# Two neighbouring DMA sums in GpSimd's queue change places, four times in a streaming encoder step

## The chip, the cores and the metric

One Trainium2 chip, one of its cores. The metric is the device time of one execution of the whole program in microseconds; lower is better. Before the change the median of three runs is 2460.01 us (2455.98 to 2460.65).

## The reference

One inference step of a two-layer streaming encoder over 640 tokens: 512 of a new prompt and 8 streams of 16. Layer A is half a SwiGLU step, differential attention, half a SwiGLU step; layer B the same with forgetting attention. All is float32.

```
def swiglu(x, w_gate, w_up, w_down):
    return (jax.nn.silu(x @ w_gate) * (x @ w_up)) @ w_down
...
x = x + 0.5 * swiglu(rms_norm(x, g_norm[l, 0]), w_ffn_gate[l, 0], w_ffn_up[l, 0], w_ffn_down[l, 0])
...
x = x + 0.5 * swiglu(rms_norm(x, g_norm[l, 2]), w_ffn_gate[l, 1], w_ffn_up[l, 1], w_ffn_down[l, 1])
```

D_MODEL is 1024 and D_FF 2816, so there are four such feed-forward stages, f = 0 to 3, each with three weight matrices of 11.5 MB. The change touches these stages alone.

## The kernel before

**Tiling.** The 2816 hidden columns are taken in 11 pairs of 128-column blocks, in groups of 2, 3, 3 and 3 pairs (`GROUPS`, g = 0 to 3). A group's work is a row of *sets* (g, s). Its first `width(g)` = 2 × pairs sets are gate (s even) and up (s odd) weights of one pair; then come four *down* sets (s = width(g) + 0 to 3), each for 256 of the 1024 output columns. For g = 0 the width is 4, so the down sets are (0,4) to (0,7), and (0,7) is followed by (1,0), the first gate set of the next group. `chain(f)` (L85) lists all sets in order. f = 0 starts at (0,2), and the last group of f = 3 has its down step in another form (`PLAIN`).

**A set.** Each set is a two-by-two block product done in seven products instead of eight, in the manner of Strassen and Winograd. Their weights are the roles W11, S1, S2, W12, S3, S4 and W22; W is a quarter of the set's weights as loaded and S a sum of quarters. Each role is split into a high and a low part of a narrower format, and TensorE makes each product as three matmul groups (L997). A gate or up set has depth 4 (quarters of 512 words per partition); a down set of the two-pair group has depth 2 (256 words), so it is half as long as others.

**Who makes what.** SyncE loads the quarters (L634 the near one, W11; L627 the first quarter, on which S1 is built; L617 the other half). GpSimd adds two of the sums by DMA with accumulation, straight from DRAM into the buffers that SyncE filled: the *first sum* makes S1 (`first_sum`, L857 to L864), the *third sum* makes S3 (`third_sum`, L866 to L873). VectorE makes S2 and S4 (`role_sum`, L2414). ScalarE casts each role to its high part (`role_high`, L1718), VectorE subtracts to get the low part (`role_low`, L2393), which counts up `w_split`. ScalarE also copies rows between PSUM banks (`copy_rows`, L1804).

**Orders.** Each engine works strictly in program order. The parts that matter around a down set `cur` (with `then` the next set):
- TensorE (`ffn_sets`, L1071): W11, S4 of the set before, S1, S2, W22 of the set before, W12, then it waits for the second row copy (`copied`) and makes S3.
- ScalarE (L1878): two row copies, W11 of `then`, S4 of `cur`, S3 of `cur` (waits for the third sum's landing, `third_added`), S1 of `then` (waits for the first sum's landing, `first_added`), the second row copy, S2 of `then`, W22 of `cur`, W12 of `then`.
- VectorE (L2691): the S4 sum of `cur`, output rows, low part W11 of `then`, low S4 of `cur`, the S2 sum of `then` (waits for `first_added` of `then`), low S3 of `cur`, low S1 and S2 of `then`, and on.
- GpSimd (`add_sums`, L855): first sums run two sets ahead of third sums. For set n of the chain it issues the third sum of n, then the first sum of n + 2.

**Waits of the two sums.** A first sum waits until SyncE's first quarter of its set has landed (`w_loaded3`) and the first sum before it has landed. A third sum waits for VectorE's S2 sum of its set, for the split of the set's W11 (its buffer is then free), and until the third sum before it has landed:

```
pool.wait_ge(w_summed, PLAN.sum[(*key, "S2")])
...
    pool.wait_ge(w_split, SPLIT[(*key, "W11")])
if PLAN.third_added[key] > 16:
    pool.wait_ge(sem("third_added"), PLAN.third_added[key] - 16)
pool.dma_start(role_source(*key, "S3"), weight_block(*key, 0, 1), accum_op=ALU.add).then_inc(sem("third_added"), 16)
```

Around the end of the two-pair group GpSimd's order is therefore: third (0,6), first (1,0), third (0,7), first (1,1), third (1,0).

Of the kernel before, what the change touches and what calls it, by code (L numbers as in the profile page):

```python
# [29 lines left out]
GROUPS = (2, 3, 3, 3)  # L30
# [33 lines left out]
DOWN_SETS = KB // 2  # L64
# [15 lines left out]
def width(g):  # L80

    return 2 * GROUPS[g]


def chain(f):  # L85

    order = []
    for g in range(len(GROUPS)):
        order += [(g, s) for s in sets_of(f, g)]
        if (f, g) not in PLAIN:  # L90
            order += [(g, width(g) + j) for j in range(DOWN_SETS)]
    return order


def is_down(g, s):
    return s >= width(g)
# [231 lines left out]
def yoco_stream_step(nc, x_prompt, x_sample, cache_a_k, cache_a_v, cache_b_k, cache_b_v, cache_b_logf,  # L328
# [4 lines left out]
    with ExitStack() as ctx:  # L333
# [12 lines left out]
        def sem(name):  # L346
            if name not in sems:
                sems[name] = ctx.enter_context(nc.semaphore(name))
            return sems[name]
# [107 lines left out]
        def role_source(f, g, s, role):  # L457

            n = depth(g, s)
            if role in ("S2", "S4"):  # L460
                return sums[:, 0:n * P].rearrange("p (k m) -> p k m", k=n)
            half, i = {"W11": (0, 0), "S3": (0, 0), "W21": (0, 1), "S1": (0, 1), "W12": (1, 0), "W22": (1, 1)}[role]
            return set_at(f, g, s)[half][:, 0:2 * n * P].rearrange("p (k i m) -> p k i m", k=n, i=2)[:, :, i, :]
# [11 lines left out]
        def weight_block(f, g, s, half, i):  # L475
            return weight_rows(f, g, s, half)[:, :, i * P:(i + 1) * P]
# [335 lines left out]
        @block.gpsimd  # L812
        def _(pool):

            pool.wait_ge(sem("ident_in"), 16)
            pool.tensor_tensor(small[:, 28:29], ident[:, 0:1], ident[:, 1:2], ALU.subtract)

            made = [0]

            def split(unit, slot, words, landed, made_by_now=None):  # L820
                pool.wait_ge(w_loaded[slot], landed)
                pool.wait_ge(w_used, unit - 1)
                pool.sem_inc(sem("pool_passed"), 1)
                pool.tensor_copy(w_hi[slot][:, 0:words], raw[slot][:, 0:words]).then_inc(w_hi_made, 1)
                pool.wait_ge(w_hi_made, made_by_now)
                pool.tensor_tensor(w_lo[slot][:, 0:words], raw[slot][:, 0:words],
                                   w_hi[slot][:, 0:words].bitcast(F32), ALU.subtract).then_inc(w_split, 1)

            def run(name, count, first=0):

                base, par, landed = BASE[name] + first, SLOT[name] + first, PLAN.landed
                pool.wait_ge(w_split, base)
                with pool.Fori(0, (count - first) // 2) as i:
                    for u in range(2):
                        split(base + i * 2 + u, (par + u) % 2, 1024, i * 16 + landed[name, first + u],
                              made_by_now=i * 2 + (made[0] + u + 1))
                made[0] += count - first

            def stage(x, b):
                if b >= 1:  # L840
                    pool.wait_ge(sem("ss_ready" + x), b)
                at = slice(b * DS + NP, b * DS + NP + DS)
                qbd = queries[x]
                pool.tensor_copy(qbd[0:64, :, 0:DS], qh[0:64, :, at]).then_inc(sem("q_staged" + x), 1)
                pool.wait_ge(sem("q_staged" + x), 2 * b + 1)
                pool.tensor_copy(qbd[64:P, :, DS:2 * DS], qh[64:P, :, at]).then_inc(sem("q_staged" + x), 1)
                pool.wait_ge(sem("q_staged" + x), 2 * b + 2)

            def spread_rows(h):

                pool.wait_ge(sem(f"row_in{h % 2}"), h // 2 * 16 + 16)
                both = FP[:, h % 2].rearrange("p c k -> p (c k)")
                pool.partition_broadcast(both, both[0:1]).then_inc(sem("rows_spread"), 1)

            def add_sums(f):  # L855

                def first_sum(at):  # L857
                    key = (f, *at)
                    if key not in PLAN.first_added:
                        return  # L860
                    pool.wait_ge(w_loaded3, PLAN.landed3[key])
                    if PLAN.first_added[key] > 16:
                        pool.wait_ge(sem("first_added"), PLAN.first_added[key] - 16)
                    pool.dma_start(role_source(*key, "S1"), weight_block(*key, 1, 1), accum_op=ALU.add).then_inc(sem("first_added"), 16)  # L864

                def third_sum(at):  # L866
                    key = (f, *at)
                    pool.wait_ge(w_summed, PLAN.sum[(*key, "S2")])
                    if (*key, "W11") not in EARLY_COUNT:
# [5 lines that stand above are left out]
                order = chain(f)  # L875
                for at in order[:2]:
                    first_sum(at)
                for n, at in enumerate(order):
                    third_sum(at)
                    if n + 2 < len(order):  # L880
                        first_sum(order[n + 2])

            add_sums(0)
            run("qkv", QKV_TILES, 2)
            pool.wait_ge(sem("qbd_clearA"), 1)
            pool.wait_ge(sem("heads_read"), 20)
            for b in range(DB):
                stage("A", b)
            pool.wait_ge(w_split, BASE["oa"])
            split(BASE["oa"], SLOT["oa"], 1024, PLAN.landed["oa", 0], made_by_now=made[0] + 1)  # L890
            made[0] += 1
            add_sums(1)
            run("kv", ROW_TILES, 2)
            split(BASE["wf"], SLOT["wf"], 1024, PLAN.landed["wf", 0], made_by_now=made[0] + 1)
            made[0] += 1
            run("kv_rest", KV_TILES - ROW_TILES)
            add_sums(2)
            run("qb", SQ_TILES, 2)
            spread_rows(0)
            pool.wait_ge(sem("qbd_clearB"), 1)  # L900
            pool.wait_ge(sem("q_read"), PAIR)
            for b in range(DB):
                stage("B", b)
                if b + 1 < PAIR:
                    spread_rows(b + 1)
            add_sums(3)
# [2505 lines left out]
```

## Time and profile before

| | |
|---|---|
| median of three runs | 2460.01 us (2455.98 to 2460.65) |
| the profiled execution | 2457.78 us |
| its span, first to last instruction | 2455.7 us |
| TensorE busy | 2402.1 us, 98% |
| VectorE busy | 1858.7 us, 76% |
| ScalarE busy | 1336.1 us, 54% |
| GpSimd busy | 544.4 us, 22% |
| DMA read from HBM | 314.98 MB, 135 GB/s over the span |
| clock granted to TensorE | 9 tenths or more of full speed in every slice |

PE is TensorE, DVE VectorE, ACT ScalarE, POOL GpSimd, SP SyncE. A timeline row gives the start in us from the span's start, the duration, engine and line, operation, what is written and read with its shape, and how many instructions the row merges; in brackets stand the engine's idle time before it and what ended that. On GpSimd a row of a DMA is the time in which it generates the transfer's descriptors, not the transfer. A row whose start lies inside the row before it was queued there and includes that wait. The profile names the weight buffers R; a source in_w_ffn_down_dram is a down set, gate and up name the others.

### The profile page before, as it was taken

The page shows a single profiled execution, that of the slowest core. Times are in us where ns is not written, and L with a number is a line of the kernel's source. Part 1 is how long each engine was busy: PE and PEld are TensorE (multiplying, and loading weights), DVE is VectorE, ACT ScalarE, POOL GpSimd, SP SyncE. Part 2 cuts the span into 40 slices and gives each one's busy share as a digit, 9 for nine tenths or more (in the row PEclk, how much of TensorE's full clock was granted, in tenths as well). Part 3 has the DMA queues.
Part 4 walks back from the last instruction along what each step waited for, and adds up shares of the span by engine and source line. Part 5 has one row for each costly group of instructions (what it writes and reads, how often), then busy time and mean ns, then how long its engine had stood idle before and what let it go on. Part 6 is the DMA issues. An engine that isn't in the chain of part 4 may idle for free. (4 is left out here: it accounts for less than half of the span.)

```text
span 2455.7 us, 48881 instructions
## 1 busy us (share of the span) xinstructions
PE 2402.1 (98%) x18377; PEld 2261.9 (92%) x18377; DVE 1858.7 (76%) x3709; ACT 1336.1 (54%) x2873; POOL 544.4 (22%) x422
## 2 busy tenths in 40 slices
PE   9899999999999999999999999999999999999998
PEld 9899999888778999999988999999996699999998
DVE  7887979422787888787925889787928878887865
ACT  6555656201785655555622655555618856555554
POOL 1222222354000121222135222222131002222210
PEclk9999999999999999999999999999999999999999
DMA  5557575333863465756523775766467544766642
GB/s 146 121 116 144 106 148 101 95 116 97 304 237 94 97 140 103 144 115 140 104 79 127 187 143 115 139 127 126 107 227 265 209 112 94 145 125 126 139 101 82
DMA packets 423237, 334.20 MB, mean 136 GB/s; under 512 B 20641, under 2 KB 383834, under 8 KB 423010
## 3 DMA queue, kind: packets, MB, share of 16 engines
q1 hardware_dynamic: 281296, 246.98, 32.2%
q0 software_dynamic: 133136, 65.82, 21.9%
q10 hardware_dynamic: 8578, 18.37, 2.1%
q8 instruction: 143, 2.34, 0.4%
q14 instruction: 84, 0.69, 0.1%
HBM read 314.98 MB, written 16.13 MB: 135 GB/s over the span
## 5 line engine op out<-in xcount | busy, mean ns | idle before, releaser
L997 PE MATMUL PS<-x_area,w_area 128*128 128x320 f32 x3096 | 483.1, 310 | 2.3 <-ACT PS L1804 2.3
L997 PEld LDWEIGHTS PS<-x_area,w_area 128*128 128x128 f32 x3096 | 461.6, 188 | 2.7 <-ACT PS L1804 2.6
L1718 ACT ACTIVATE w_area<-R 128x512 fp32r<-128x512 f32 (+2 forms) x583 | 325.5, 567 | 204.9 <-DVE R L2414 92.3
L2393 DVE TENSOR_TENSOR w_area<-R,w_area 128x512 fp32r<-128x512 f32 (+2 forms) x583 | 357.7, 615 | 87.1 <-ACT w_area L1718 86.5
L2393 DVE TENSOR_TENSOR r_area<-R,r_area 128x512 fp32r<-128x512 f32 (+2 forms) x437 | 265.8, 617 | 94.4 <-ACT r_area L1718 88.8
L1804 ACT ACTIVATE PS<-PS 128x320 f32<-128x320 f32 x438 | 178.3, 416 | 215.6 <-PE PS L997 189.9
L997 PE MATMUL PS<-r_area,w_area 128*128 128x320 f32 x1584 | 266.4, 311 | 10.7 <-ACT PS L1804 6.2
L1718 ACT ACTIVATE r_area<-R 128x512 fp32r<-128x512 f32 (+2 forms) x437 | 247.7, 567 | 47.2 <-DVE R L2414 20.2
L997 PEld LDWEIGHTS PS<-r_area,w_area 128*128 128x128 f32 x1584 | 239.1, 188 | 18.3 <-ACT PS L1804 11.2
L1226 PE MATMUL PS<-w_area,xn_hi 128*128 128x512 f32 x800 | 251.5, 396 | 0.5 <-DVE xT L2578 0.3
L997 PE MATMUL PS<-r_area 128*128 128x320 f32 x1392 | 236.5, 311 | 2.2 <-DVE r_area L2648 1.8
L997 PE MATMUL PS<-k_area,r_area 128*128 128x320 f32 x1440 | 236.9, 310 | 0.7 <-DVE k_area L2648 0.6
L997 PEld LDWEIGHTS PS<-k_area,r_area 128*128 128x128 f32 x1440 | 217.5, 188 | 1.5 <-DVE k_area L2648 1.2
L997 PEld LDWEIGHTS PS<-r_area 128*128 128x128 f32 x1392 | 212.1, 189 | 6.1 <-DVE r_area L2648 3.6
L2414 DVE TENSOR_TENSOR R<-R 128x512 f32<-128x512 f32 (+2 forms) x289 | 177.9, 616 | 2.2
L997 PE MATMUL PS<-v_area,w_area 128*128 128x320 f32 x960 | 175.7, 311 | 3.5 <-DVE w_area L2393 1.7
L1226 PEld LDWEIGHTS PS<-w_area,xn_hi 128*128 128x128 f32 x800 | 146.8, 188 | 30.1 <-DVE xT L2578 1.2
L997 PE MATMUL PS<-x_area,r_area 128*128 128x320 f32 x1032 | 165.4, 309 | 0.0
L1226 PE MATMUL PS<-w_area,xn_lo 128*128 128x512 f32 x400 | 156.3, 391 | 0.0
L997 PEld LDWEIGHTS PS<-x_area,r_area 128*128 128x128 f32 x1032 | 154.9, 188 | 0.1
L997 PEld LDWEIGHTS PS<-v_area,w_area 128*128 128x128 f32 x960 | 149.1, 188 | 6.1 <-ACT PS L1804 3.4
L864 POOL DMA_DIRECT2D R<-in_w_ffn_up_dram x43 | 55.8, 1297 | 380.9 <-DMA R<-in_w_ffn_up_dram 258.4
(348 smaller groups left out, 4152.6 us busy)
## 6 DMA issues: line engine op xcount, KB each, us to landing
R<-in_w_ffn_up_dram SPq DMA_DIRECT2D x45, 512.0 KB, 5.2
R<-in_w_ffn_gate_dram SPq DMA_DIRECT2D x43, 512.0 KB, 5.1
R<-in_w_ffn_up_dram SPq DMA_DIRECT2D x86, 256.0 KB, 4.1
R<-in_w_ffn_up_dram POOLq DMA_DIRECT2D x86, 256.0 KB, 4.8
R<-in_w_ffn_gate_dram SPq DMA_DIRECT2D x82, 256.0 KB, 4.6
R<-in_w_ffn_gate_dram POOLq DMA_DIRECT2D x81, 256.0 KB, 5.5
R<-in_w_ffn_down_dram SPq DMA_DIRECT2D x52, 384.0 KB, 3.9
R<-in_w_ffn_down_dram SPq DMA_DIRECT2D x88, 192.0 KB, 3.7
```

Of the source, the lines that this page charges most:

```text
L864: pool.dma_start(role_source(*key, "S1"), weight_block(*key, 1, 1), accum_op=ALU.add).then_inc(sem("first_added"), 16)
L997: last = pe.matmul(PS[:, bank, 0:HT], a[:, k, :], b, start=(start and opens), stop=(k == n - 1 and a is lo), skip_group_check=True)
L1226: last = pe.matmul(PS[:, t, :], x[:, k, cols], a[s][:, w], start=(k == 0 and x is xn_hi and a is w_hi), stop=(k == KB - 1 and x is xn_lo))
L1718: act.activation(role_parts(f, g, s, role)[0], role_source(f, g, s, role), ACT.Copy).then_inc(sem("early_cast") if key in EARLY_COUNT else ...
L1804: act.activation(PS[:, to, 0:HT], PS[:, of, 0:HT], ACT.Copy).then_inc(sem("copied"), 1)
L2393: dve.tensor_tensor(lo, role_source(f, g, s, role), hi.bitcast(F32), ALU.subtract).then_inc(sem("early_split") if key in EARLY_COUNT else ...
L2414: dve.tensor_tensor(*at, ALU.add).then_inc(w_summed, 1)
```

## The change

In each f, the third sum of (0,7) is put ahead of the first sum of (1,0). `ahead` holds just (0,7): a down set of a group of two pairs whose number is at least width + 3. Its third sum is issued one step earlier in the loop, right behind the third sum of (0,6), and skipped in its own step. Around the end of the group the order becomes: third (0,6), third (0,7), first (1,0), first (1,1), third (1,0). The waits inside both functions are unchanged, and so are the order and the waits of every other engine.

```diff
                 order = chain(f)
                 for at in order[:2]:
                     first_sum(at)
+                ahead = [at for at in order[1:] if is_down(*at) and GROUPS[at[0]] == 2 and at[1] >= width(at[0]) + DOWN_SETS - 1]
                 for n, at in enumerate(order):
-                    third_sum(at)
+                    if at not in ahead:
+                        third_sum(at)
+                    if n + 1 < len(order) and order[n + 1] in ahead:
+                        third_sum(order[n + 1])
                     if n + 2 < len(order):
                         first_sum(order[n + 2])
```

## Rows read from the trace of the kernel before

**Rows 1.** The page's part on busy time: us, share of the span, instructions.
```profile
PE 2402.1 (98%) x18377; PEld 2261.9 (92%) x18377; DVE 1858.7 (76%) x3709; ACT 1336.1 (54%) x2873; POOL 544.4 (22%) x422
```

**Rows 2.** Waits of TensorE: who waited for whom, us in all, times, longest.
```profile
PE PS L997 <- ACT PS L1804: 11.9, 11, 2.3
```

**Rows 3.** TensorE's timeline: start, us, instruction, count [idle before it <- what ended it].
```profile
103.17 1.15 PE L997 MATMUL PS<-r_area,w_area 128*128 128x320 f32 x6 [0.76 <-ACT PS L1804]
...
891.63 1.14 PE L997 MATMUL PS<-r_area,w_area 128*128 128x320 f32 x6 [0.69 <-ACT PS L1804]
...
902.03 2.03 PE L997 MATMUL PS<-v_area,w_area 128*128 128x320 f32 x12 [0.46 <-ACT PS L1804]
...
1434.19 0.70 PE L997 MATMUL PS<-v_area,w_area 128*128 128x320 f32 x3 [1.21 <-ACT PS L1804]
...
2097.78 1.14 PE L997 MATMUL PS<-r_area,w_area 128*128 128x320 f32 x6 [0.96 <-ACT PS L1804]
```

**Rows 4.** ScalarE's timeline around set (0,7) of f = 3.
```profile
2089.29 0.42 ACT L1718 ACTIVATE w_area<-R 128x256 fp32r<-128x256 f32 x1 [2.56 <-DMA R<-in_w_ffn_down_dram]
...
2096.46 0.42 ACT L1718 ACTIVATE w_area<-R 128x256 fp32r<-128x256 f32 x1 [2.22 <-DMA R<-in_w_ffn_down_dram]
2096.78 0.61 ACT L1718 ACTIVATE r_area<-R 128x512 fp32r<-128x512 f32 x1
2097.30 0.42 ACT L1804 ACTIVATE PS<-PS 128x320 f32<-128x320 f32 x1
```

**Rows 5.** VectorE's timeline of the same stretch.
```profile
2087.78 0.42 DVE L2414 TENSOR_TENSOR R<-R 128x256 f32<-128x256 f32 x1
...
2095.49 0.69 DVE L2414 TENSOR_TENSOR R<-R 128x512 f32<-128x512 f32 x1
...
2096.91 0.42 DVE L2393 TENSOR_TENSOR w_area<-R,w_area 128x256 fp32r<-128x256 f32 x1 [0.73 <-ACT w_area L1718]
```

**Rows 6.** GpSimd's timeline of the same stretch: its DMA issues.
```profile
2082.97 1.20 POOL L873 DMA_DIRECT2D R<-in_w_ffn_down_dram  x1 [0.50 <-DVE R L2414]
2089.72 1.28 POOL L864 DMA_DIRECT2D R<-in_w_ffn_gate_dram  x1 [5.56 <-DMA R<-in_w_ffn_gate_dram]
2090.48 1.75 POOL L873 DMA_DIRECT2D R<-in_w_ffn_down_dram  x1
2095.78 1.33 POOL L864 DMA_DIRECT2D R<-in_w_ffn_up_dram  x1 [3.56 <-DMA R<-in_w_ffn_up_dram]
```

**Rows 7.** GpSimd's timeline at the same place of f = 0, 1 and 2.
```profile
94.81 1.28 POOL L864 DMA_DIRECT2D R<-in_w_ffn_gate_dram  x1 [3.92 <-DVE w_area L2393]
95.56 1.75 POOL L873 DMA_DIRECT2D R<-in_w_ffn_down_dram  x1
...
883.04 1.28 POOL L864 DMA_DIRECT2D R<-in_w_ffn_gate_dram  x1 [3.48 <-DMA R<-in_w_ffn_gate_dram]
884.05 1.49 POOL L873 DMA_DIRECT2D R<-in_w_ffn_down_dram  x1
...
1425.78 1.28 POOL L864 DMA_DIRECT2D R<-in_w_ffn_gate_dram  x1 [4.35 <-DMA R<-in_w_ffn_gate_dram]
1426.53 1.75 POOL L873 DMA_DIRECT2D R<-in_w_ffn_down_dram  x1
```

**Rows 8.** VectorE's timeline, f = 0, 1 and 2: the S2 sum of (0,7).
```profile
94.66 0.42 DVE L2414 TENSOR_TENSOR R<-R 128x256 f32<-128x256 f32 x1
...
883.33 0.42 DVE L2414 TENSOR_TENSOR R<-R 128x256 f32<-128x256 f32 x1
...
1425.04 0.43 DVE L2414 TENSOR_TENSOR R<-R 128x256 f32<-128x256 f32 x1
```

**Rows 9.** Line L864, the first sum of (1,0) alone, f = 0 and f = 3.
```profile
DMA to landing us min/median/max: 5.5/5.5/5.5
...
DMA to landing us min/median/max: 5.0/5.0/5.0
```

**Rows 10.** Line L873, all 146 third sums, from issue to landing.
```profile
DMA to landing us min/median/max: 3.2/5.7/8.3
```

## The prediction

> **What bounds the kernel now.** Start with the busy shares. TensorE works in 2402.1 of 2455.7 us [rows 1]: time can be won only where it stands still. The list of waits says who it stands still for: the largest entry is ScalarE's copy of PSUM rows at L1804, 11 waits, 11.9 us in all [rows 2]. Then the timeline of TensorE says where these waits lie. Number the feed-forward stages f = 0 to 3. In each, one such wait stands in set (0,7), the last down set of the two-pair group, ahead of its S3 product: 0.76, 0.69, 1.21 and 0.96 us [rows 3], together 3.62 us. The other seven entries lie in other sets. So 3.62 us is all that TensorE can win at the place of the change.
>
> Why does it wait? Read f = 3 backwards. The copy ran at 2097.30 because ScalarE, which works in program order, held the cast of S3 until 2096.46, where a DMA landed (2.22 us idle), and then made the cast of S1 of set (1,0) [rows 4]. VectorE made S3's low half at 2096.91 [rows 5]. The landed DMA is the third sum of (0,7). GpSimd issued it at 2090.48, behind the first sum of (1,0), issued at 2089.72, which had waited 5.56 us for its own quarter of weights [rows 6]. The start itself is not the whole matter: the first sum occupies GpSimd until 2091.00, and the third sum, 1.75 us long in its row where such a one alone takes 1.20, is done at 2092.23. The two are generated one behind the other.
>
> **The change, part by part.** Nothing is computed, added or removed: in each f, one pair of neighbours in GpSimd's order changes places, the first sum of (1,0) and the third sum of (0,7), with the waits of each. Four swaps in all. SyncE's order is the same.
>
> (a) When can the third sum start? It needs the sum S2 of (0,7) from VectorE, the split of W11 and the landing of the third sum of (0,6). In f = 1 the sum ends at 883.33 + 0.42 = 883.75 and the third sum starts at 884.05 [rows 7, 8]: 0.30 from event to start. The S2 sum ends at 95.08, 883.75, 1425.47 and 2088.20 [rows 5, 8]; in f = 3 the third sum of (0,6) lands later, about 2089.27, as the cast at 2089.29 shows [rows 4]. So the third sum would start at 95.38, 884.05, 1425.77 and 2089.57, against 95.56, 884.05, 1426.53 and 2090.48 [rows 6, 7]. The start gains 0.18, 0, 0.76 and 0.91 us. Generated alone in 1.20 us [rows 6] it would be done at 96.58, 885.25, 1426.97 and 2090.77, against 97.31, 885.54, 1428.28 and 2092.23: earlier by 0.73, 0.29, 1.31 and 1.46.
>
> (b) What does the first sum lose? It is now generated behind the third, 1.28 us [rows 6, 7]: done at 97.86, 886.53, 1428.25 and 2092.05 against 96.09, 884.32, 1427.06 and 2091.00, later by 1.77, 2.21, 1.19 and 1.05. It landed 5.5 us after its start in f = 0 and 5.0 in f = 3 [rows 9], that is 4.2 and 3.7 after the end of its row; for f = 1 and 2 I take 4.0 between them. New landings: 102.06, 890.53, 1432.25 and 2095.75.
>
> (c) What is late next? The first sum feeds work that stands ahead of the row copy and of S3's low half: on ScalarE the cast of S1 of (1,0) (0.52 us until the copy starts) and then the copy, 0.42 [rows 4]; on VectorE the S2 sum of (1,0), 0.69 us [rows 5], stands ahead of S3's low half, 0.42 [rows 5]. So TensorE cannot go on sooner than 0.69 + 0.42 and some 0.04 for the signals, 1.15 us, after the first sum lands. Today the same end comes 1.34 us after the third sum lands (2097.78 against about 2096.44). The third sum will be in by then: it would be ahead in GpSimd's queue by one generation. So the first sum takes over as the last to come, and TensorE goes on at 103.21, 891.68, 1433.40 and 2096.90. Against 103.17, 891.63, 1434.19 and 2097.78 [rows 3] this is -0.04, -0.05, 0.79 and 0.88 us: 1.6 us won in all.
>
> (d) Behind the swapped pair on GpSimd stands the first sum of (1,1), at 2095.78 after 3.56 us idle [rows 6]; a pair that is done at 2092.05 instead of 2092.23 does not touch it. The next stall fed by this queue is in f = 1 at 902.03, 0.46 us [rows 3], in the S3 product of (1,0); whatever f = 1 gained would be lost there, another reason to count it as nothing. The other three stages show no stall there, and what they win stays, since TensorE is what bounds the stages that follow.
>
> Rule against row. The rows show that generation has a price: 1.28 us for the leading sum, and the following one ends 1.2 us behind it [rows 6]. The Trainium skill, "DMA: Bandwidth & Descriptors", section "Anatomy of one DMA — SWDGE (gpsimd) path", puts generation as "small, variable" and a DMA at 2.0 us plus bytes over 436e3. By that page, as an estimate, a first sum of 262144 bytes costs the third behind it only 0.6 us and the swap would win about 4 × 0.6 = 2.4 us, inside the band of the forecast below. The sum here goes by the rows.
>
> The sum against the profiled execution: 2457.8 - 1.6 = 2456.2 us (its span is 2455.7, with 2.1 around it). The median of the runs shown is 2460.0, 2.2 above that execution; I give the forecast on the median's scale: 2460.0 - 1.6 = **2458.4 us**. The runs of before lie over 4.7 us, so about 0.2% (4.9 us) is what a measurement of this kernel can tell from no change.
>
> **Bounds.** At best all four stalls vanish and the third sums that follow come no later: 3.6 us. At worst the first sum, which now meets the set loads that SyncE issues meanwhile, lands as late as the slowest third sum, 8.3 us after its issue [rows 10] (the median is 5.7). With a start 0.75 us behind the third sum (96.13, 884.80, 1426.52, 2090.32) and 1.15 us after landing, TensorE would go on at 105.58, 894.25, 1435.97 and 2099.77: later than now by 2.4, 2.6, 1.8 and 2.0, 8.8 us in all. I take the value of (b), since that is the row of the very transfer, moved by some 1 to 2 us.
>
> **Rivals.** (1) The late first sum: the wait that takes the place of the one removed. Place: VectorE's S2 sum of (1,0) and ScalarE's S1 cast, both ahead of S3's work. It decides from the landing at which a stage ends as late as now: 103.17 - 1.15 - 96.13 = 5.9 us after the first sum's start in f = 0, and likewise 5.7, 6.5 and 6.3 in the others; (b) stands at 5.9, 5.7, 5.7 and 5.4. At 7.0 us, midway between the median and the slowest third sum, it costs 8.8 - 4 × 1.3 = 3.6 us: 2463.6. For it speaks that sums of this kind take up to 8.3 us here [rows 10]; against it that the first sums took 5.0 to 5.5 [rows 9]. (2) Hidden anyway: the two transfers fill the queue as one, so the last one lands when the last one did. Then only the shorter tail, 1.34 - 1.15 = 0.19 us each, is won: 0.8 us, 2459.2. For it: they are served from one queue. Against it: in f = 2 and 3 GpSimd sat idle until the first sum's quarter had come, time that the third sum now uses. (3) Clean: all stalls go, 3.6 us, 2456.4; the f = 0 and 1 start times speak against it. (4) The change does not act: no pair is swapped, 2460.0. The condition names exactly set (0,7) of each f, so this has next to no chance.
>
> **How the numbers follow.** Forecast as worked out (0.5 to 3 us won): 0.55. Rival 2: 0.2. Rival 1: 0.14, of which the part beyond 4.9 us is perhaps half, as its worst is 8.8. Rival 3, with anything beyond it that the traces do not show: 0.10. Rival 4: 0.01. Even the ceiling of 3.6 us is under 0.2%, so "faster" needs the scatter of the medians (or a side effect) on its side: 0.11. "Slower" takes half of rival 1: 0.07. "Same": 0.82. The range: from 2454.8, the ceiling with 1.6 us of scatter, to 2461.8, half of rival 1 with none; what is left out is rival 1's upper half and rare scatter, under 2 in 10.
>
> **What would show it.** In the changed profile GpSimd's rows stand as third sum (a down issue) then first sum (a gate issue), at the four places; the third starts about 0.8 us earlier against the S2 sum in f = 2 and 3, and not in f = 0 and 1. ScalarE's idle time before the S3 cast goes from 2.22 us to under 1 in f = 3, and a new wait, on the gate DMA, appears before the S1 cast. TensorE's stall in (0,7) is nearly gone in f = 2 and 3 and stays near 0.7 in f = 0 and 1; the one at 902.03 stays. I am wrong if the stalls of f = 0 and 1 also go (then the first sum does not hold the S3 work as (c) says), if any of the four grows by over half a microsecond (rival 1), or if the time moves by more than 5 us, since then something outside the four sets has moved.

## The result: 0.2% slower, and the profile after

The changed kernel takes 2465.35 us (median of 20 runs, 2458.14 to 2469.39), the kernel before 2460.33 us (20 runs, 2454.35 to 2468.55) on the same chip. The ratio is 1.0022 with a 95% interval of 1.0014 to 1.0030: 3.4 to 7.4 us slower. The forecast was 2458.4 us and its range ended at 2461.8. It was wrong: rival 1, the late first sum, is what happened. The profiled execution took 2464.94 us, its span 2462.9 against 2455.7.

The page's part on busy time says at once that TensorE does no more work than before [rows 1]:

```profile
PE 2402.8 (98%) x18377; PEld 2261.7 (92%) x18377; DVE 1855.6 (75%) x3709; ACT 1336.2 (54%) x2873; POOL 544.5 (22%) x422
```

The loss is idle time, and TensorE's list of waits shows a new leader. In it stand who waits, for whom, us in all, times and the longest. Before, the row copy led with 11.9 us [rows 2] and the low part of a down set's weights (`role_low`, now L2397) stood at 5.9 us:

```profile
PE PS L1001 <- DVE w_area L2397: 13.4, 18, 3.2
PE PS L1001 <- ACT PS L1808: 9.8, 8, 2.3
```

TensorE's timeline places them. The lines of the changed kernel below the change are numbered four higher than before, so L1001 is L997. These rows answer to [rows 3]:

```profile
103.47 1.11 PE L1001 MATMUL PS<-r_area,w_area 128*128 128x320 f32 x6 [1.74 <-DVE w_area L2397]
...
114.26 2.02 PE L1001 MATMUL PS<-k_area,w_area 128*128 128x320 f32 x12 [0.88 <-ACT PS L1808]
...
893.28 1.11 PE L1001 MATMUL PS<-r_area,w_area 128*128 128x320 f32 x6 [1.22 <-DVE w_area L2397]
...
904.78 2.04 PE L1001 MATMUL PS<-v_area,w_area 128*128 128x320 f32 x12 [1.59 <-ACT PS L1808]
...
1439.73 0.67 PE L1001 MATMUL PS<-v_area,w_area 128*128 128x320 f32 x3 [3.22 <-DVE w_area L2397]
...
2104.87 1.11 PE L1001 MATMUL PS<-r_area,w_area 128*128 128x320 f32 x6 [1.26 <-DVE w_area L2397]
...
2115.09 2.02 PE L1001 MATMUL PS<-v_area,w_area 128*128 128x320 f32 x12 [0.31 <-ACT PS L1808]
```

Two places, not one. Ahead of S3 of (0,7) the four stalls are 1.74, 1.22, 3.22 and 1.26 us, 7.44 in all, where 3.62 stood. In set (1,0), one set further, they are 0.88, 1.59, 0 and 0.31, 2.78 in all, where 0.46 stood. Together that is 3.82 + 2.32 = 6.1 us of the 7.2 by which the spans differ.

**GpSimd** did what the diff says. Its timeline of f = 3, beside [rows 6]:

```profile
2096.41 1.19 POOL L873 DMA_DIRECT2D R<-in_w_ffn_down_dram  x1 [4.34 <-DVE R L2418]
2097.11 1.82 POOL L864 DMA_DIRECT2D R<-in_w_ffn_gate_dram  x1
2104.15 1.30 POOL L864 DMA_DIRECT2D R<-in_w_ffn_up_dram  x1 [5.22 <-DMA R<-in_w_ffn_gate_dram]
2104.90 1.87 POOL L873 DMA_DIRECT2D R<-in_w_ffn_gate_dram  x1
```

The third sum (0,7) starts on VectorE's sum, the first sum of (1,0) is queued behind it. What the forecast had not looked at is the third row: the first sum of (1,1) used to wait for its own quarter of weights [rows 6]; now it waits for the *landing* of the first sum of (1,0), because first sums wait for each other. The third sum of (1,0) depends on that landing twice: it stands behind this first sum, and it needs VectorE's S2 sum of (1,0), which waits for the same landing.

How late the first sum landed is one line of the view of line L864, one sum at a time, f = 0 to 3 (compare [rows 9], 5.5 and 5.0 us):

```profile
DMA to landing us min/median/max: 7.0/7.0/7.0
...
DMA to landing us min/median/max: 6.5/6.5/6.5
...
DMA to landing us min/median/max: 8.2/8.2/8.2
...
DMA to landing us min/median/max: 6.5/6.5/6.5
```

From the end of their rows these are 5.2, 4.7, 6.4 and 4.7 us, where 4.2, 4.0, 4.0 and 3.7 stood. SyncE's timeline of f = 2 shows what they now meet. L617 is the 512 KB load of the other half of the same set (1,0):

```profile
1429.89 0.37 SPq L634 DMA_DIRECT2D R<-in_w_ffn_gate_dram  x1
1430.86 0.37 SPq L627 DMA_DIRECT2D R<-in_w_ffn_up_dram  x1
1432.39 0.37 SPq L617 DMA_DIRECT2D R<-in_w_ffn_gate_dram  x1
1439.61 0.37 SPq L634 DMA_DIRECT2D R<-in_w_ffn_up_dram  x1
```

The same half load in SyncE's timeline of the kernel before, where the first sum's row ends at 1427.06 [rows 7]:

```profile
1428.65 0.37 SPq L617 DMA_DIRECT2D R<-in_w_ffn_gate_dram  x1
```

In the changed kernel the first sum's row ends at 1430.24 + 1.82 = 1432.06, 0.33 us ahead of the issue of this load; in the other stages the lead is 0.23, 0.23 and 0.09. Before, it was 1.5 to 2.5 us: the sum had a start on the load. Now both travel together, and in f = 2 the load lands 6.4 us after its issue, at 1438.8, the sum at 1438.48.

**ScalarE and VectorE** of f = 3 then show the tail, the cast of S1 ahead of the row copy, the S2 sum ahead of S3's low half. First ScalarE:

```profile
2103.64 0.63 ACT L1722 ACTIVATE r_area<-R 128x512 fp32r<-128x512 f32 x1 [2.67 <-PE PS L1001]
2104.18 0.42 ACT L1808 ACTIVATE PS<-PS 128x320 f32<-128x320 f32 x1
```

and VectorE:

```profile
2103.70 0.69 DVE L2418 TENSOR_TENSOR R<-R 128x512 f32<-128x512 f32 x1 [1.74 <-issue]
2104.30 0.42 DVE L2397 TENSOR_TENSOR w_area<-R,w_area 128x256 fp32r<-128x256 f32 x1
```

The sum landed at 2103.62; both engines wake at 2103.64 and 2103.70, and TensorE goes on at 2104.87, 1.25 us after the landing. In all four stages it is 1.25. The releaser in brackets is not the DMA here (a product for ScalarE, "issue" for VectorE); the time of the landing tells it. In f = 2 ScalarE's row names the DMA itself, with 4.17 us idle.

**The clock** adds a little in f = 2. This is the windows view of the 10 us after the 3.22 us stall; behind the busy times stand the granted clock, the DMA share and GB/s:

```profile
1439.73:1449.73 10.00, 10.00 (x58) 10.00 (x59) 6.28 (x13) 3.68 (x9) 3.19 (x3) 0.83 0.86 170
```

The same 10 us before had a granted clock of 1.00. At 0.83 instead of 1, 1.7 us of work is lost: the record shows 3.4 us at 1.2 GHz, from 1440.7. One such stretch after another stall, at 74.1 us, is in the profile of before alone, so this does not explain the difference of the spans. Nor does the clock explain the slower median: the mean granted clock is 0.9962 over the 20 executions of the changed kernel and 0.9964 over the 84 of the kernel before that were taken beside the experiments.

### The profile page after: what moved, and what is told of

Its sections match the earlier page's. It is cut to its first block and busy times, and to the rows that moved or that the text cites. A ratio compares the mean times of both kernels' runs of the same rounds, so it can differ in the third digit from the quotient of the medians.

```text
span 2462.9 us, 48881 instructions
## 1 busy us (share of the span) xinstructions
PE 2402.8 (98%) x18377; PEld 2261.7 (92%) x18377; DVE 1855.6 (75%) x3709; ACT 1336.2 (54%) x2873; POOL 544.5 (22%) x422
## 5 line engine op out<-in xcount | busy, mean ns | idle before, releaser
L1001 PE MATMUL PS<-x_area,w_area 128*128 128x320 f32 x3096 | 482.5, 309 | 2.3 <-ACT PS L1808 2.3
L1001 PEld LDWEIGHTS PS<-x_area,w_area 128*128 128x128 f32 x3096 | 461.0, 188 | 2.9 <-ACT PS L1808 2.6
L2397 DVE TENSOR_TENSOR w_area<-R,w_area 128x512 fp32r<-128x512 f32 (+2 forms) x583 | 358.0, 616 | 90.8 <-ACT w_area L1722 90.0
L2397 DVE TENSOR_TENSOR r_area<-R,r_area 128x512 fp32r<-128x512 f32 (+2 forms) x437 | 265.8, 617 | 89.2 <-ACT r_area L1722 83.9
L1001 PE MATMUL PS<-r_area,w_area 128*128 128x320 f32 x1584 | 265.9, 311 | 11.2 <-DVE w_area L2397 9.4
L1001 PEld LDWEIGHTS PS<-r_area,w_area 128*128 128x128 f32 x1584 | 239.1, 188 | 18.4 <-ACT PS L1808 12.3
L1001 PE MATMUL PS<-r_area 128*128 128x320 f32 x1392 | 237.0, 312 | 3.3 <-DVE r_area L2652 2.8
L1001 PE MATMUL PS<-k_area,r_area 128*128 128x320 f32 x1440 | 236.9, 309 | 0.7 <-DVE k_area L2652 0.6
L1001 PEld LDWEIGHTS PS<-r_area 128*128 128x128 f32 x1392 | 212.4, 189 | 7.2 <-DVE r_area L2652 4.5
L1001 PEld LDWEIGHTS PS<-k_area,r_area 128*128 128x128 f32 x1440 | 217.6, 188 | 1.5 <-DVE k_area L2652 1.2
L1001 PE MATMUL PS<-v_area,w_area 128*128 128x320 f32 x960 | 176.0, 311 | 7.5 <-DVE w_area L2397 4.0
L1001 PE MATMUL PS<-x_area,r_area 128*128 128x320 f32 x1032 | 165.6, 309 | 0.0
L1001 PEld LDWEIGHTS PS<-v_area,w_area 128*128 128x128 f32 x960 | 149.3, 188 | 10.4 <-ACT PS L1808 7.7
L1001 PEld LDWEIGHTS PS<-x_area,r_area 128*128 128x128 f32 x1032 | 154.9, 188 | 0.3 <-DVE x_area L2449 0.3
L864 POOL DMA_DIRECT2D R<-in_w_ffn_up_dram x43 | 55.7, 1295 | 385.7 <-DMA R<-in_w_ffn_up_dram 255.1
```

Of the source, the lines that this page charges most:

```text
L1001: last = pe.matmul(PS[:, bank, 0:HT], a[:, k, :], b, start=(start and opens), stop=(k == n - 1 and a is lo), skip_group_check=True)
L2397: dve.tensor_tensor(lo, role_source(f, g, s, role), hi.bitcast(F32), ALU.subtract).then_inc(sem("early_split") if key in EARLY_COUNT else ...
```

## The experiments

All ratios are to the kernel before, on the same chip. "(0,7)" and "(1,0)" below mean TensorE's stalls at these two sets, in the order f = 0 to 3, from its timeline; before they sum to 4.1 us, after to 10.2.

### 1. Take the late first sum out of S3's way

In the changed kernel, around (0,7), ScalarE makes the row copy ahead of the cast of S1 of (1,0), and VectorE S3's low half ahead of the S2 sum of (1,0). The moves are made only at `closes`, which is true at (0,7) alone.

```diff
+                    closes = is_down(*cur) and GROUPS[cur[0]] == 2 and then is not None and not is_down(*then)
+                    if closes:
+                        copy_rows(f, *cur, 2)
                     if then is not None:
                         role_high(f, *then, "S1")
-                    if n >= 2:
+                    if n >= 2 and not closes:
                         copy_rows(f, *cur, 2)
...
+                    if closes:
+                        role_low(f, *cur, "S3")
                     if then is not None and is_down(*cur):
                         dve.wait_ge(w_split, SPLIT[(f, *cur, "S4")])
                         role_sum(f, *then, "S2")
...
-                    if n and not third_first(f, cur):
+                    if n and not third_first(f, cur) and not closes:
                         role_low(f, *cur, "S3")
```

> The changed kernel, and in set (0,7) VectorE makes S3's low half ahead of the S2 sum of (1,0), and ScalarE copies the row ahead of the S1 cast of (1,0). Nothing of S3's work stands behind the late first sum any more. Theory A (the first sum lands late, and TensorE waits for it only through these two orders): the stalls in (0,7), 1.74, 1.22, 3.22 and 1.26 us in the changed kernel, fall under 0.3 each, and the time comes 5 us or more below the changed kernel's. Theory B (the late first sum also holds GpSimd's next issues, first sum of (1,1) and third sum of (1,0)): the stalls in (0,7) go too, but TensorE stops again at S3 of (1,0), by 1.5 to 2.8 us in f = 0, 1 and 3, and the time stays 2 to 4 us above the kernel before.

Measured: 2457.55 us against 2457.66, ratio 0.9993 (0.9982 to 1.0003). The loss is gone. The first sums still land late, 5.0, 5.4, 5.2 and 6.4 us after their rows, but TensorE has no stall ahead of S3 of (0,7) in any stage. ScalarE's timeline of f = 2 shows why: its idle time stands behind the copy now, not ahead of it.

```profile
1434.74 0.42 ACT L1808 ACTIVATE PS<-PS 128x320 f32<-128x320 f32 x1 [0.60 <-PE PS L1001]
1437.21 1.42 ACT L1722 ACTIVATE r_area<-R 128x512 fp32r<-128x512 f32 x2 [2.05 <-DMA R<-in_w_ffn_gate_dram]
```

At (1,0) smaller stalls are left, 0.88, 0.53, 1.10 and 0.71, and one of 0.79 a little earlier in f = 3: 4.0 us, what before has in all. A second effect goes with it. With S3 split early its buffer is free early, and SyncE loads the near quarter of (1,1) at 1435.46, where the changed kernel did so at 1439.61 (SyncE's timeline above):

```profile
1435.46 0.37 SPq L634 DMA_DIRECT2D R<-in_w_ffn_up_dram  x1
```

The third sums of (1,0) then take 7.4, 6.6, 7.2 and 6.8 us from start to landing, against 9.2, 9.9, 9.4 and 8.6 in the changed kernel and 7.3, 8.3, 7.3 and 7.1 before. That they meet less traffic is the likely reason; no run separates it.

### 2. The same two moves without the swap

> The kernel before with the same two moves on VectorE and ScalarE, GpSimd's order untouched. Both theories: the stalls in (0,7), 0.76, 0.69, 1.21 and 0.96 us, shrink by some 0.4 us each, since the row copy (0.42 us) no longer follows the landing of the third sum; the time falls by about 1.5 us, 0.06%, hardly to be told from none. If it rises, the two moves themselves cost something and e1 has to be read with that.

Measured: 2456.05 us against 2457.66, ratio 0.9991 (0.9982 to 1.0001), not to be told from run 1. TensorE's stalls are 0, 0, 0.47 and 1.16 at (0,7), and 1.25 at (1,0) in f = 1: 2.9 us where before has 4.1, so they shrank in sum about as expected, but not evenly. With the coupling at (0,7) gone, these two runs show neither a cost nor a gain of the swap beyond their scatter of some 2.5 us.

### 3. The late first sum alone

The order of before is kept; the first sum of (1,0) waits for what the third sum (0,7) waits for, and then for four tiny subtractions on GpSimd, about as long as the generation it would stand behind. The kernel computes four numbers more, which nothing uses.

```diff
+                    if at == (1, 0):
+                        pool.wait_ge(w_summed, PLAN.sum[(f, 0, 7, "S2")])
+                        pool.wait_ge(sem("third_added"), PLAN.third_added[f, 0, 6])
+                        for i in range(4):
+                            pool.tensor_tensor(small[:, 9:10], ident[:, 0:1], ident[:, 1:2], ALU.subtract).then_inc(w_hi_made, 1)
+                            made[0] += 1
+                            pool.wait_ge(w_hi_made, made[0])
                     pool.dma_start(role_source(*key, "S1"), weight_block(*key, 1, 1), accum_op=ALU.add).then_inc(sem("first_added"), 16)
```

> The kernel before with its order on GpSimd, first sum of (1,0) and then third sum of (0,7), but the first sum waits for what the third sum waits for and then for four small GpSimd operations that stand in for the 1.2 us in which the third sum would be generated. So the first sum is issued as late as in the changed kernel, with nothing ahead of it in its queue. Theory T (the later time is what hurts: it meets SyncE's 512 KB half load): from the end of its row it takes 4.6 us or more to land, as in the changed kernel (5.2, 4.7, 6.4, 4.7). Theory Q (standing behind the third sum in GpSimd's queue hurts): it lands in 3.7 to 4.2 us, as in the kernel before. In both, the third sum comes later than before and the time rises, by 4 to 10 us.

Measured: 2475.23 us against 2457.66, ratio 1.0073 (1.0061 to 1.0085). The first sum lands 5.4, 6.1, 4.4 and 3.6 us after the end of its row: as theory T wants in f = 0 and 1, between the two in f = 2, as theory Q wants in f = 3. Run 6 takes this up. The third sum is late too, since it stands behind. The stalls at (0,7) are 3.42, 4.37, 3.36 and 4.17 us, 15.3 in all, 11.7 more than before. Two of these rows, f = 1 and f = 2:

```profile
897.92 1.44 PE L1004 MATMUL PS<-r_area,w_area 128*128 128x320 f32 x4 [4.37 <-ACT PS L1811]
...
1443.81 0.70 PE L1004 MATMUL PS<-v_area,w_area 128*128 128x320 f32 x3 [3.36 <-ACT PS L1811]
```

The median grew by 17.6 us; the profiled execution, the fastest of the six, took 2471.12, 13.3 above the profiled one of before. The windows of 10 us that start at the ends of the four stalls (TensorE alone, its granted clock behind the count):

```profile
105.55:115.55 10.00, 10.00 (x68) 1.00 0.84 175
897.92:907.92 10.00, 10.00 (x54) 0.77 0.85 167
1443.81:1453.81 10.00, 10.00 (x58) 0.83 0.75 156
2110.97:2120.97 10.00, 10.00 (x58) 0.84 0.82 165
```

In three of the four the clock is lower (in f = 1 and 3 it fell before the stall had ended), and 2.3 + 1.7 + 1.6 = 5.6 us of work is lost. That makes 17.3 us with the stalls, more than the 13.3; but the profile of before has two stretches of 3.4 us at 1.2 GHz, at 1954.8 and 2442.9 us, that this one has not, up to 1.7 us each. So the stall is the larger part of the price, the clock the smaller.

### 4. Hold the half load back, changed kernel

```diff
+                    if key[1:] == (1, 0):
+                        sp.wait_ge(sem("first_added"), PLAN.first_added[key])
                     set_load(*key, (1,))
```

> The changed kernel, and SyncE holds its 512 KB half load of set (1,0) until the first sum of (1,0) has landed. Theory T (that load's packets drag out the first sum): the first sum lands 3.6 to 4.2 us after the end of its row and the stalls in (0,7) fall to the 0.8, 0.7, 0.4 and 0.1 us or so that were forecast. Theory Q: 4.6 us or more as in the changed kernel, stalls unchanged. The held load may cost time of its own later, in set (1,0) and (1,1), so the landing and the stalls of (0,7) decide, not the time.

Measured: 2464.55 us against 2457.66, ratio 1.0025 (1.0015 to 1.0036). The first sums land 4.5, 4.5, 4.4 and 4.2 us after their rows, where the changed kernel has 5.2, 4.7, 6.4 and 4.7: the long one is gone, but they are not back at the figure of the forecast. The load's share is then 0.7, 0.2, 2.0 and 0.5 us (1.0, 0.7, 0.7 and 0.5 beside the second profile of the changed kernel, run 8); the rest, 0.3 to 0.5, has another cause. Stalls at (0,7) fall from 7.4 to 4.1 us (1.24, 1.19, 0.93, 0.72), and come back at (1,0), 6.0 us (1.87, 1.94, 1.55, 0.66), where the changed kernel has 2.8. The likely reason is that the held load now travels with the first sum of (1,1) and the third of (1,0), which takes 10.2 us from start to landing in f = 0. Holding the load back moved the wait one set on; it did not remove it.

### 5. Only VectorE's half of run 1

> The changed kernel with only VectorE's half of e1: S3's low half of (0,7) is made ahead of the S2 sum of (1,0), while ScalarE still copies the row behind the S1 cast of (1,0). If either order is enough to hold TensorE until the late first sum has landed, the stalls in (0,7) stay within 0.2 us of the changed kernel's, ended by the row copy instead of the low half, and the time stays at 1.002 of the kernel before. If VectorE's order alone made the stall, they vanish as in e1.

Measured: 2463.16 us against 2460.08, ratio 1.0011 (1.0001 to 1.0022). TensorE still stalls at (0,7), 1.40, 1.52, 1.87 and 1.25 us, and not at (1,0). The releaser has changed from VectorE to the row copy, as its row of f = 0 shows:

```profile
103.18 0.99 PE L1001 MATMUL PS<-r_area,w_area 128*128 128x320 f32 x5 [1.40 <-ACT PS L1808]
```

The stalls are not within the 0.2 us that were expected (1.74, 1.22, 3.22 and 1.26 in the changed kernel), but they stay, so ScalarE's order alone is enough to hold TensorE. That VectorE's alone would be enough was not run; in the changed kernel its low half is what ends all four stalls, so it is the later of the two there. The stalls at (1,0) are gone: VectorE's half frees the buffer early, so that SyncE issues the near quarter of (1,1) in f = 0 at 100.48 instead of 103.35, and TensorE comes to (1,0) later by its stall at (0,7). Which of the two does it was not separated.

### 6. Run 3 with the half load held back

> e3 (first sum late, nothing of GpSimd's ahead of it) with SyncE's 512 KB half load of (1,0) held until the first sum has landed. Theory T (the overlap with that load is what lengthens it): from the end of its row to landing 3.4 to 4.1 us in all four stages, where e3 had 5.4, 6.1, 4.4 and 3.6. Theory Q: no change against e3.

Measured in one execution: 2467.1 us. From start to landing of the first sum, f = 0 to 3, first run 3 and then this one (views of the sum's line):

```profile
DMA to landing us min/median/max: 6.7/6.7/6.7
...
DMA to landing us min/median/max: 7.4/7.4/7.4
...
DMA to landing us min/median/max: 5.7/5.7/5.7
...
DMA to landing us min/median/max: 5.0/5.0/5.0
```

```profile
DMA to landing us min/median/max: 5.0/5.0/5.0
...
DMA to landing us min/median/max: 5.2/5.2/5.2
...
DMA to landing us min/median/max: 4.5/4.5/4.5
...
DMA to landing us min/median/max: 4.9/4.9/4.9
```

Same transfer, same lateness, the one neighbour away: 1.7, 2.2, 1.2 and 0.1 us quicker. From the end of its row it lands after 3.7, 3.95, 3.2 and 3.5 us. The overlap with the half load is what lengthens the landing in f = 0 to 2. Stalls at (0,7) are 1.98, 1.36, 1.28 and 5.56 us. The last belongs to a third sum of (0,7) that came late: ScalarE idles 7.23 us until its DMA lands. The transfer was not slow, 4.9 us from start to landing; GpSimd began late. Its timeline of f = 3, first in run 3 and then in this one, has

```profile
2102.20 1.25 POOL L868 TENSOR_TENSOR small<-cst 128x1 f32<-128x1 f32 x4 [8.02 <-issue]
...
2095.30 1.42 POOL L870 TENSOR_TENSOR small<-cst 128x1 f32<-128x1 f32 x4 [8.18 <-DMA R<-in_w_ffn_up_dram]
```

These are the four subtractions. VectorE's S2 sum, which they wait for, had ended at 2099.50 and 2091.17, 2.7 and 4.1 us earlier; in f = 0 to 2 of both runs they begin 0.25 us after it. So f = 3 of both runs has a delay of its own, whose cause is open. It also tells why the load makes no difference there: in run 3 the half load was issued at 2102.70, 2.5 us ahead of the end of the sum's row (2105.22), and not at the same time as in the other stages, and had landed by 2107.3.

### 7. The moves of run 1 at all three short pairs of neighbours, without the swap

`closes` loses its last condition, so (0,5) and (0,6) take part too.

> The kernel before, with the two moves of e2 at all three down sets (0,5), (0,6) and (0,7) of the two-pair group. At (0,6) and (0,7) S3's low half no longer stands behind the next S2 sum (0.34 us) and the row copy no longer behind the landing: 0.3 to 0.5 us less at each stall, 2 to 4 us in all over e2's single place, if the third sums do not come later by it. Against: the next set's S2 sum is made 0.3 us later, and the third sum that waits for it with it, which gives the gain back one set later: then no difference from e2.

Measured: 2455.14 us against 2460.08, ratio 0.9979 (0.9970 to 0.9987). Run 12 repeats it.

### 8. The changed kernel once more

> The changed kernel once more, on the chip of these runs: time 1.001 to 1.003 of the kernel before; first sum of (1,0) 4.5 us or more from the end of its row to landing in most stages; stalls in (0,7) of 1.2 us or more. It tells how far one profile of it stands for the others.

Measured: 2466.31 us (9 runs) against 2458.83, ratio 1.0032 (1.0021 to 1.0042). First sums land 5.5, 5.2, 5.1 and 4.6 us after their rows. Stalls are 2.03, 1.74, 1.85 and 1.20 at (0,7) and 0.25, 0.75, 0.85 and 0.32 at (1,0): 9.0 us, 4.9 more than before, with no stretch of lower clock behind any of them. The 3.22 us of f = 2 was one execution's; the rest repeats.

### 9. The moves of run 7 in the changed kernel

> The two moves of e7 at (0,5), (0,6) and (0,7), on the changed kernel's GpSimd order. If the swap has nothing to give once S3's work is uncoupled (the third sum's earlier landing is no longer the last thing, the first sum's later one delays the third sum of (1,0)), the time is e7's or 1 to 3 us above it: 0.998 to 1.000 of the kernel before. If the earlier third sum pays once the coupling is gone, it is 1 to 2 us below e7.

Measured: 2461.48 us against 2458.83, ratio 1.0012 (1.0001 to 1.0023). At (0,7) almost nothing is left, but (1,0) stalls twice in a stage. For f = 1 TensorE's timeline has

```profile
901.02 2.03 PE L1001 MATMUL PS<-x_area,r_area 128*128 128x320 f32 x12 [0.80 <-ACT PS L1808]
907.14 2.04 PE L1001 MATMUL PS<-v_area,w_area 128*128 128x320 f32 x12 [1.45 <-ACT PS L1808]
```

and all four stages together 8.2 us. Beside run 7, and just so beside its repetition (run 12, upper end of the interval 1.0002), the swap costs here even with the coupling gone; run 1 beside run 2 did not show it.

### 10 and 11. The moves at the down sets of every group, without the swap

`closes` is then `is_down(*cur) and then is not None`.

> The kernel before, with the two moves of e7 at the down sets of every group. Each down set of a three-pair group is half as long again and TensorE has next to no stall in them (one of 0.25 us in a group), so nothing more is won: the time is e7's within 2 us, 0.997 to 0.9990 of the kernel before. The S2 sum made 0.4 us later in each set could bring new stalls of a few tenths.

> e10 once more, beside e7 on the same chip: 0.996 to 0.998 of the kernel before. If it comes out at e7's ratio, the moves in the three-pair groups are worth nothing and e10's first figure was scatter; if it stays 0.0008 or more under it in both measurements, they are worth something.

Measured: 2450.94 us against 2458.83, ratio 0.9971 (0.9957 to 0.9984), and again 2449.54 against 2459.88, ratio 0.9961 (0.9945 to 0.9976). This version is faster than both kernels, twice; that nothing more would be won in the three-pair groups was wrong. The busy time of run 10, the page's part, shows that part of the gain was never idle time in the profile:

```profile
PE 2396.5 (98%) x18377; PEld 2258.2 (92%) x18377; DVE 1855.0 (76%) x3709; ACT 1333.9 (54%) x2873; POOL 543.9 (22%) x422
```

The same 18377 matmuls are "busy" for 5.6 us less than before [rows 1]. Up to 3.4 us of that are the two stretches of lower clock at 1954.8 and 2442.9 us, which before has and this execution has not. The rest is in the three-pair groups: set side by side, start for start, the matmuls gain 0.4 to 0.5 us once in ten of the eleven such groups and keep it, 4.8 us in all, where before showed only small waits or none, such as this one, which run 10 does not have:

```profile
195.12 1.12 PE L997 MATMUL PS<-r_area,w_area 128*128 128x320 f32 x6 [0.24 <-DVE w_area L2393]
```

In TensorE's waits the row copy falls from 11.9 us [rows 2] to 4.4, and the low part takes some of it over:

```profile
PE PS L997 <- DVE w_area L2396: 9.8, 11, 1.9
PE PS L997 <- ACT PS L1804: 4.4, 3, 2.3
```

### 12. Run 7 once more

> e7 once more: 0.997 to 0.999 of the kernel before. Its first figure of 0.9979 was 4.9 us for stalls that its profile shows to shrink by about one; a figure nearer 1 would say that the first was partly scatter.

Measured: 2457.44 us against 2459.88, ratio 0.9993 (0.9984 to 1.0002). The gain of run 7 came out smaller and not clear of none, so the short sets alone are not shown to bring anything. Run 11, beside this one on the same chip, is clearly below it (0.9945 to 0.9976): what runs 10 and 11 win is, in the main, in the three-pair groups.

## Why the forecast was wrong, by its steps

**What bounds the kernel** was right for this change: TensorE's work stayed the same and the stalls decided. That "time can be won only where it stands still" was too strong as a reading of the profile: run 10 won at least 2.2 us that stood there as busy.

**Step (a)** held. The third sum started on VectorE's sum, was generated alone in 1.19 us and landed earlier by its measure, 2.7 to 3.0 us after its row instead of 4.2 to 4.8.

**Step (b)** is the step that failed. The first sum's row did end behind the third's as worked out. But I then took its landing, 4.2, 4.0, 4.0 and 3.7 us after the row's end, from where it had stood, "since that is the row of the very transfer, moved by some 1 to 2 us". It measured 5.2, 4.7, 6.4 and 4.7 (5.5, 5.2, 5.1 and 4.6 in run 8). A landing belongs to a transfer *and what travels with it*, and those 1 to 2 us were the whole lead that the sum had on SyncE's half load. Run 6 against run 3 shows this for f = 0 to 2 by taking only the load away; in the changed kernel itself (run 4) the load accounts for 0.2 to 2.0 us of the 0.7 to 2.4 by which the landing grew. From start to landing the forecast said 5.9, 5.7, 5.7 and 5.4 against bounds of 5.9, 5.7, 6.5 and 6.3 at which a stage breaks even: f = 0 and f = 1 had no slack at all. Measured were 7.0, 6.5, 8.2 and 6.5, beyond the bound in every stage. The trace of before had the warning in SyncE's timeline, a row that I did not set beside GpSimd's.

The Trainium skill, "DMA: Bandwidth & Descriptors", section "Queues, rings and completion order", says that each of the DMA engines takes turns between the queues that have work for it, packet by packet. By that rule a sum of one queue that starts together with a load of another shares with it until one is done. The trace agrees as far as landings can show it: in f = 0 to 3 the sums landed only 0.3 to 1.4 us before the half load that was issued behind them.

**Step (c)** was right in kind and nearly in size. The first sum became the last to come, through just the two pieces of work it named, and TensorE went on 1.25 us after the landing where it said 1.15. Run 1 shows that this coupling carries the loss: with both pieces moved, the stalls at (0,7) are gone although the sums are as late as ever. Run 5 shows that ScalarE's piece alone would be enough.

**Step (d)** failed too. It held that a pair done at 2092.05 instead of 2092.23 "does not touch" the first sum of (1,1). It compared the end of *generation*; the next first sum waits for a *landing*, and so does VectorE's S2 sum of (1,0), ahead of the third sum of (1,0). Against the moment at which TensorE came to S3 of (0,7), that landing had moved by 2.6, 2.6, 3.9 and 2.1 us. The third sum of (1,0) then took 9.2, 9.9, 9.4 and 8.6 us from start to landing where before had 7.3, 8.3, 7.3 and 7.1. The waits on the landing do not explain this longer flight, since run 1 has them too and shows 7.4, 6.6, 7.2 and 6.8; what run 1 lacks is SyncE's near quarter of (1,1) at that moment, whose buffer S3's late split frees late; that it is this load was not shown by itself. (1,0) stalls in three stages, 2.3 us more than before. It is the wait that I had listed myself, under the waits of the two sums.

**Rival 1** was the right mechanism, with the right place, and its 3.6 us would have given 2463.6 against 2465.35. The range left its upper half out by giving it 0.14. The argument against it was the one figure of (b); with f = 0 and f = 1 at their break-even points and the possible gain no more than 1.6 us, a loss deserved at least even chances. The signs named at the end of the forecast did their work: three of the four stalls grew by over half a microsecond (0.98, 0.53 and 2.01), and three in run 8.

**What stays open.** Whether the swap costs anything once the coupling is gone: runs 1 and 2 do not show it, run 9 beside 7 and 12 says 0.2 to 0.3%. Why the landings of run 4 stay 0.3 to 0.5 us above those of before with the load away (4.5, 4.5, 4.4 and 4.2 against 4.2, 4.0, 4.0 and 3.7); the third sum, now close ahead in the same queue, may take part in it and was not separated. What held GpSimd's subtractions back in f = 3 of runs 3 and 6. Why 0.4 to 0.5 us are won in a three-pair group that showed 0.24 us of waiting. The 20 executions of the changed kernel lie over 11 us, and the clock takes part in that (the 17 executions of before with a mean granted clock of 0.995 took 2460.3 us on average, the 12 with 0.998 took 2456.3); this is why the single stretches of lower clock are not charged to the change.

## What to carry to other kernels

When a transfer is moved in one queue, set its new time beside the issues of the *other* queues before reusing its old time to landing: losing a lead of 1.5 to 2.5 us on a 512 KB load, and coming behind another sum, cost 0.7 to 2.4 us of landing here. Ask of each later wait whether it is on an issue or on a landing. And where an engine in program order has work that TensorE needs behind work that waits for a late DMA, try moving the needed piece ahead before speeding up the DMA: here that brought 0.3 to 0.4% (runs 10 and 11), mostly at sets where the profile showed hardly a stall, while issuing the DMA earlier lost 0.2%.

## What the runs showed of the hardware that was not expected

A busy TensorE can hide waiting. In run 10 the span fell by 6.8 us against the profile of before, and 5.6 us of that stood there as busy time, up to 3.4 of them clock. That short waits between matmuls are counted as work, their ends being modelled, is my reading of it; the starts of the matmuls, compared one by one, showed the gain and its places.

The length of a stall alone does not tell whether the clock falls to 1.2 GHz behind it. After 3.42 us in f = 0 of run 3 the granted clock stayed at 1.00 over the next 10 us; after 3.36 us in f = 2 of the same run it was 0.83, and so it was after only 1.87 us in f = 2 of run 5:

```profile
1437.09:1447.09 10.00, 10.00 (x58) 0.83 0.81 149
```
